# Norms of a two-stage transformer kernel: one over the root on 64 columns, spread over the partitions by small products

## The chip, the core and the metric

The kernel runs on one core of a Trainium2 chip. A core has a matrix engine (TensorE, PE in the profile; its weight loads are PEld), a vector engine (VectorE, DVE), a scalar engine (ScalarE, ACT), GpSimd (POOL) and a sync engine (SyncE, SP), with 16 DMA engines behind the queues. Each engine runs its own instructions in order and waits for the others by semaphores. The metric is the device time of one execution in microseconds (us); the number quoted is the median of the runs shown.

## The reference

One sequence of T = 256 tokens with D = 1024 features passes a first block (a modulated norm, a mixer of a Fourier part and a gated delta rule over tokens and a context, a gated feed-forward with a convolution) and then two layers (attention, retention and a linear recurrence side by side, then a feed-forward). Between all of these stand root-mean-square norms over the 1024 features of each token:

```
def rms_norm(x, g):
    xf = x.astype(jnp.float32)
    y = xf * lax.rsqrt(jnp.mean(xf * xf, axis=-1, keepdims=True) + EPS)
    return (y * g.astype(jnp.float32)).astype(x.dtype)
```

There are 13 of them in the kernel, numbered k = 0 to 12: 0 and 1 on the two inputs, then pairs. The first of a pair (2, 4, 6, 8, 10, and 12 alone at the end) normalises the output of a branch, which is then scaled and added to x ("residual norm"); the second (3, 5, 7, 9, 11) normalises the new x for the next branch ("modulate norm").

## The kernel before

Activations lie transposed: `[P, KT, T]`, that is 128 partitions, 8 blocks of 128 features, 256 tokens. Weights stream in through a ring of slots in chunks of 128x2048 fp32 (1 MB, `raw`), by SP's queue. ACT copies each chunk to a rounded `w_hi` (L1059) and DVE subtracts to get `w_lo` (L1590, 2.29 us a chunk); PE then multiplies in three products per tile (`mm3`, L342 to L344), 48 matmuls a chunk. There are two buffers of `w_hi` and `w_lo`, so the preparation of chunk n+2 starts when chunk n is done. The order of the work on each engine is written out by hand; the only things that order engines against each other are semaphores.

A norm runs over four engines' worth of code. ACT squares two blocks at a time (`square`, L1100, 128x512). For each of the four pairs of blocks PE multiplies by `omean`, a 128x128 matrix with 1/1024 in every place (`norm_part`, L446), so that after eight products all 128 partitions of PSUM bank 7 hold the mean of squares of all 256 tokens: the sum over the partitions and its spreading over them are one step. ACT takes the root of 128x256 with eps (`root`, L1105, tile `std`). DVE takes the reciprocal of 128x256 (L1619 in `rs`, L1637 in `root_done`, tile `rstd`) and multiplies by it: `residual` (L1667 from PSUM, then L1675 into x), `modulate` (L1653, with L1654 for the low part behind ACT's L1125), `rs` for norms 0 and 1 (L1624), and L1967 for norm 3. Each of the first three parts of a residual norm stands between two weight chunks in PE's order; the fourth stands behind the last chunk.

Behind a norm PE has filler work, in its order ahead of the next thing that waits: `keep_warm` (L457, products of 512 columns whose results nobody reads: 4 before and 4 behind norms 7 and 11, likewise around norm 9, 2 in front of norm 3, 2 behind norm 5) and `ada_mm` (L467, products with the modulation weights, 16 matmuls of 32 weight columns for each 1 MB half that POOL's queue loads into one of two buffers; the next load into a buffer waits until it has been used). After a modulate norm PE's next chunk (`mod_chunk`, `up_chunk`) waits block by block for the modulated activations.

Of the kernel before, what the change touches and what calls it, by code (L numbers as in the profile page):

```python
# [90 lines left out]
def build_program(nc, io, layers=LAYERS):  # L91
# [6 lines left out]
    with ctx:  # L98
# [239 lines left out]
        def _(pe):  # L338
# [1242 lines left out]
        def _(dve):  # L1581
# [159 lines left out]
            def conv_kv(c):  # L1741
                dve.wait_ge(S("evicted"), c + 3)
                for i in range(3):
                    for b in (2 * c, 2 * c + 1):
# [721 lines left out]
```

## Time and profile before

| | |
|---|---|
| median of 3 runs | 1807.72 us (1801.07 to 1809.67) |
| the profiled execution | 1812.65 us, of which its span 1810.8 us |
| mean granted TensorE clock | 0.981 |
| PE busy | 1709.5 us (94%) |
| DVE busy | 1097.9 us (61%) |
| ACT busy | 811.7 us (45%) |
| reciprocals of 128x256 | 13, each 1.75 us |
| means by L446 | 13 x 8 matmuls |

The span is from the first to the last instruction; the time of a run lies 1.85 us above it here. A matmul of fp32 data is recorded as two (x16 rows for the 8 matmuls of a norm). Busy time of PE counts a matmul from its start to its modelled end, so that 94% is no measure of what PE could not do. Idle time in brackets behind a row is that of the engine before it, with what ended it.

### The profile page before, as it was taken

The page shows a single profiled execution, that of the slowest core. Times are in us where ns is not written, and L with a number is a line of the kernel's source. Part 1 is how long each engine was busy: PE and PEld are TensorE (multiplying, and loading weights), DVE is VectorE, ACT ScalarE, POOL GpSimd, SP SyncE. Part 2 cuts the span into 40 slices and gives each one's busy share as a digit, 9 for nine tenths or more (in the row PEclk, how much of TensorE's full clock was granted, in tenths as well). Part 3 has the DMA queues.
Part 4 walks back from the last instruction along what each step waited for, and adds up shares of the span by engine and source line. Part 5 has one row for each costly group of instructions (what it writes and reads, how often), then busy time and mean ns, then how long its engine had stood idle before and what let it go on. Part 6 is the DMA issues. An engine that isn't in the chain of part 4 may idle for free.

```text
span 1810.8 us, 34649 instructions
## 1 busy us (share of the span) xinstructions
PE 1709.5 (94%) x15394; PEld 1607.6 (89%) x15394; DVE 1097.9 (61%) x1367; ACT 811.7 (45%) x1050; POOL 34.2 (2%) x68
## 2 busy tenths in 40 slices
PE   6998788899989799999999999999999999999997
PEld 4797688789979599999999799979999999979997
DVE  4466753579953554477785664565547778666463
ACT  3245413343333344445754444435364575445352
POOL 0000000000000000000000000000000000000000
PEclk8999999999989899999999999999999999999999
DMA  9676442555558553445455355535444445535551
GB/s 401 241 269 255 160 182 94 188 212 175 173 189 300 210 171 138 140 163 185 165 187 181 112 195 188 188 115 185 134 150 160 163 166 186 188 113 188 196 198 71
DMA packets 45210, 329.32 MB, mean 182 GB/s; under 512 B 5008, under 2 KB 5008, under 8 KB 5392
## 3 DMA queue, kind: packets, MB, share of 16 engines
q1 hardware_dynamic: 35712, 258.63, 41.2%
q0 software_dynamic: 9216, 67.11, 9.8%
q8 instruction: 114, 1.87, 0.4%
q10 hardware_dynamic: 144, 1.51, 0.2%
q14 instruction: 24, 0.20, 0.0%
HBM read 326.18 MB, written 1.05 MB: 181 GB/s over the span
## 4 chain that ended last, share of the span: by engine, by line
PE 76%; DVE 11%; ACT 7%; DMA 4%; issue 1%; SPq 0%; POOL 0%; ACTq 0%; DVEq 0%
PE ps L342 19%; PE ps L343 19%; PE ps L344 19%; DVE w_lo L1590 4%; PE ps L395 4%; ACT w_hi L1059 3%; PE ps L467 3%; DMA ada_raw<-ada 2%; PE ps L446 2%; DMA raw<-stream 2%; PE ps L627 1%; PE ps L638 1%; DVE rstd L1637 1%; DVE rsq L2309 1%; DVE x L1675 1%
## 5 line engine op out<-in xcount | busy, mean ns | idle before, releaser
L1590 DVE TENSOR_TENSOR w_lo<-raw,w_hi 128x2048 fp32r<-128x2048 f32 x207 | 474.4, 2292 | 501.4 <-ACT w_hi L1059 501.0
L342 PE MATMUL ps<-act_hi,w_hi 128*128 128x256 f32 x2672 | 757.7, 284 | 18.1 <-DVE act_lo L1632 5.0
L343 PE MATMUL ps<-act_lo,w_hi 128*128 128x256 f32 x2672 | 745.7, 279 | 0.0
L344 PE MATMUL ps<-act_hi,w_lo 128*128 128x256 f32 x2672 | 745.6, 279 | 0.0
L1059 ACT ACTIVATE w_hi<-raw 128x2048 fp32r<-128x2048 f32 (+1 forms) x229 | 421.8, 1842 | 568.9 <-PE ps L344 559.4
L342 PEld LDWEIGHTS ps<-act_hi,w_hi 128*128 128x128 f32 x2672 | 505.6, 189 | 29.1 <-issue 16.5
L343 PEld LDWEIGHTS ps<-act_lo,w_hi 128*128 128x128 f32 x2672 | 505.2, 189 | 1.1 <-issue 0.2
L344 PEld LDWEIGHTS ps<-act_hi,w_lo 128*128 128x128 f32 x2672 | 504.4, 189 | 0.0
L342 PE MATMUL ps<-mlp_hi,w_hi 128*128 128x256 f32 x512 | 142.9, 279 | 0.4
L343 PE MATMUL ps<-mlp_lo,w_hi 128*128 128x256 f32 x512 | 141.4, 276 | 0.0
L344 PE MATMUL ps<-mlp_hi,w_lo 128*128 128x256 f32 x512 | 141.4, 276 | 0.0
L342 PEld LDWEIGHTS ps<-mlp_hi,w_hi 128*128 128x128 f32 x512 | 96.1, 188 | 1.1 <-DVE w_lo L1598 1.0
L2006 DVE SCALAR_TENSOR_TENSOR gacc<-gpad,vectors,gacc 128x256 f32<-128x256 f32 x176 | 84.6, 481 | 19.8 <-ACT gacc L1327 14.7
L343 PEld LDWEIGHTS ps<-mlp_lo,w_hi 128*128 128x128 f32 x512 | 96.1, 188 | 0.2
L344 PEld LDWEIGHTS ps<-mlp_hi,w_lo 128*128 128x128 f32 x512 | 96.2, 188 | 0.0
L467 PE MATMUL ps<-ada_raw,silu_c_wide 128*32 128x256 f32 x1024 | 67.4, 400 | 21.4 <-DMA ada_raw<-ada 21.3
L395 PE MATMUL ps<-h_up,raw 128*128 128x256 f32 x352 | 82.3, 386 | 1.6 <-ACT h_up L1317 1.3
L395 PEld LDWEIGHTS ps<-h_up,raw 128*128 128x128 f32 x352 | 65.4, 192 | 13.2 <-ACT h_up L1317 3.0
L467 PEld LDWEIGHTS ps<-ada_raw,silu_c_wide 128*32 128x32 f32 x1024 | 30.1, 113 | 47.8 <-DMA ada_raw<-ada 27.4
L342 PE MATMUL ps<-w_hi,act_hi 128*128 128x256 f32 x256 | 72.2, 282 | 0.0
L344 PE MATMUL ps<-w_hi,act_lo 128*128 128x256 f32 x256 | 71.3, 279 | 0.0
L343 PE MATMUL ps<-w_lo,act_hi 128*128 128x256 f32 x256 | 71.3, 278 | 0.0
(404 smaller groups left out, 2053.5 us busy)
## 6 DMA issues: line engine op xcount, KB each, us to landing
raw<-stream SPq DMA_DIRECT2D x233, 1024.0 KB, 4.9
ada_raw<-ada POOLq DMA_DIRECT2D x64, 1024.0 KB, 6.9
ada_f<-ada SPq DMA_DIRECT2D x4, 1024.0 KB, 12.8
ada_a<-ada SPq DMA_DIRECT2D x3, 1024.0 KB, 19.8
consts_stage<-consts_a SPq DMA_DIRECT2D x1, 1728.0 KB, 33.7
consts_stage<-consts_b ACTq DMA_DIRECT2D x1, 1472.0 KB, 8.9
x<-xT SPq DMA_DIRECT2D x1, 1024.0 KB, 5.8
xc<-ctxT SPq DMA_DIRECT2D x1, 1024.0 KB, 7.8
```

The lines of the kernel that those rows point to most:

```text
L342: mm(out, ah, bh, start=first, stop=False, skip_group_check=shared)
L343: mm(out, ah, bl, start=False, stop=False, skip_group_check=shared)
L344: return mm(out, al, bh, start=False, stop=last, skip_group_check=shared)
L395: mm(ps[:, bank, 0:T], raw[:, slot, k * P:(k + 1) * P], h_up[:, k, :], start=k == 0, stop=k == KT - 1)
L446: last = mm(ps[:, 7, 0:T], omean, sq[:, b, :], start=b == 0, stop=b == KT - 1)
L467: last = mm(ps[strip:strip + 32, bank, c * T:(c + 1) * T], cs_wide[:, k, 32 - 3 * j:64 - 3 * j], ada_raw[:, c, k * T:(k + 1) * T], start=j ...
L627: last = mm(ps[r:r + 64, INV_BANK[q], j * 64:(j + 1) * 64], B01[d][r:r + 64, t0 + j // 4, j % 4, r:r + 64], Tm[r:r + 64, q, j, :], start=T ...
L638: last = mm(ps[r:r + 64, INV_BANK[q], j * 32:(j + 1) * 32], Uc[r:r + 64, q, j, :], half(X[r:r + 64, q, j, :], d, 1 << lvl), start=True, st ...
L1059: act_(w_hi[:, s2, o:CH], raw[:, s4, o:CH], ACT.Copy).then_inc(S("hi_ready"), 1)
L1590: tt(w_lo[:, s2, :], raw[:, s4, :], w_hi[:, s2, :].bitcast(f32), ALU.subtract).then_inc(S("lo_ready"), 1)
L1637: nc.vector.reciprocal(rstd[:, :], std[:, :]).then_inc(S("norm_rstd"), 1)
L2006: ins = stt(acc, src, w, acc, ALU.mult, ALU.add)
```

## The change

The 256 tokens are cut in four quarters of 64. In `norm_part` each block is multiplied in four matmuls of 32 weight columns and 64 data columns; quarter i goes to PSUM partitions 32i to 32i+31, columns 0 to 63 of bank 7. Every partition of a strip of 32 then holds the means of that strip's quarter. Root and reciprocal work on 128x64 (`std[:, 0:64]`, `std[:, 64:128]`). Then four matmuls, each with one column of the identity (the column of partition 32i) repeated 128 times as weights, take row 32i of the reciprocals and spread it over all 128 partitions, to columns 256 + 64i of bank 7. These four stand in PE's order right behind the last part of the mean, with a wait for DVE's reciprocal ahead of them. Residual norms and norms 0 and 1 copy the 128x256 result to `rstd` first (`root_done`); modulate norms read it in PSUM (`root_row`). Four semaphores are merged into two (`eps_set` and `cs_ready` into `consts_set`; `conv` and `y_ready` into `kqv_done`), and PE's second norm waits for `norm_rstd` in place of `norm_std`.

```diff
-                    last = mm(ps[:, 7, 0:T], omean, sq[:, b, :], start=b == 0, stop=b == KT - 1)
+                    for i in range(4):
+                        last = mm(ps[32 * i:32 * i + 32, 7, 0:64], omean[:, 0:32], sq[:, b, 64 * i:64 * i + 64],
+                                  start=b == 0, stop=b == KT - 1, skip_group_check=True)
                 if q == 3:
                     last.then_inc(S("norm_ms"), 1)
+                    pe.wait_ge(S("norm_inv"), k + 1)
+                    for i in range(4):
+                        last = mm(ps[:, 7, T + 64 * i:T + 64 * i + 64], ident[:, 32 * i:32 * i + 1].to_broadcast([P, P]), std[:, 64:128],
+                                  start=True, stop=True)
+                    last.then_inc(S("norm_row"), 1)
...
             norm(0, norm_sq1)
-            pe.wait_ge(S("norm_std"), 1)
+            pe.wait_ge(S("norm_rstd"), 1)
...
-                act_(std[:, :], ps[:, 7, 0:T], ACT.Sqrt, bias=eps[:, :]).then_inc(S("norm_std"), 1)
+                act_(std[:, 0:64], ps[:, 7, 0:64], ACT.Sqrt, bias=eps[:, :]).then_inc(S("norm_std"), 1)
...
+            def root_row(k):
+
+                dve.wait_ge(S("norm_std"), k + 1)
+                nc.vector.reciprocal(std[:, 64:128], std[:, 0:64]).then_inc(S("norm_inv"), 1)
+                dve.wait_ge(S("norm_row"), k + 1)
+                return ps[:, 7, T:2 * T]
+
+            def root_done(k):
+
+                row = root_row(k)
+                copies[0] += 1
+                nc.vector.tensor_copy(rstd[:, :], row).then_inc(S("norm_rstd"), 1)
+                dve.wait_ge(S("norm_rstd"), copies[0])
...
-            def root_done(k):
-
-                dve.wait_ge(S("norm_std"), k + 1)
-                nc.vector.reciprocal(rstd[:, :], std[:, :]).then_inc(S("norm_rstd"), 1)
-                dve.wait_ge(S("norm_rstd"), k + 1)
...
-                root_done(k)
-                pipe(m, lambda b: stt(tmp[:, b, :], src[:, b, :], g[:, b:b + 1], rstd[:, :], ALU.mult, ALU.mult),
+                row = root_row(k)
+                pipe(m, lambda b: stt(tmp[:, b, :], src[:, b, :], g[:, b:b + 1], row, ALU.mult, ALU.mult),
```

PE's order around norms 6 and 7 (end of the mixer of the first layer), before; L342 to L344 are the last products of the last weight chunk, L446 the means, L457 `keep_warm`, and the last rows the first chunk of the feed-forward:

```order
L344 MATMUL ps<-act_hi_53,w_lo 128x256
L446 MATMUL ps<-s_136,consts_common 128x256 x4
L457 MATMUL ps<-consts_common 128x512 x4
L446 MATMUL ps<-s_136,consts_common 128x256 x8
L457 MATMUL ps<-consts_common 128x512 x4
L342 MATMUL ps<-act_hi_54,w_hi 128x256
```

The same place in the changed kernel; L447 are the means, L453 the four spreading products (they wait for DVE), L464 `keep_warm`:

```order
L344 MATMUL ps<-act_hi_53,w_lo 128x256
L447 MATMUL ps<-s_136,consts_common 32x64 x16
L453 MATMUL ps<-std,consts_common 128x64 x4
L464 MATMUL ps<-consts_common 128x512 x4
L447 MATMUL ps<-s_136,consts_common 32x64 x32
L453 MATMUL ps<-std,consts_common 128x64 x4
L464 MATMUL ps<-consts_common 128x512 x4
L342 MATMUL ps<-act_hi_54,w_hi 128x256
```

Each `keep_warm` now stands behind a wait for the reciprocal. The same happens to `ada_mm` around norms 4 and 5; before (L467 is `ada_mm`):

```order
L446 MATMUL ps<-sq_down,consts_common 128x256 x2
L467 MATMUL ps<-ada_raw,silu_c_wide 32x256 x32
L446 MATMUL ps<-s_136,consts_common 128x256 x8
L467 MATMUL ps<-ada_raw,silu_c_wide 32x256 x16
L457 MATMUL ps<-consts_common 128x512 x2
```

and after (L474 is `ada_mm`):

```order
L447 MATMUL ps<-sq_down,consts_common 32x64 x8
L453 MATMUL ps<-std,consts_common 128x64 x4
L474 MATMUL ps<-ada_raw,silu_c_wide 32x256 x32
L447 MATMUL ps<-s_136,consts_common 32x64 x32
L453 MATMUL ps<-std,consts_common 128x64 x4
L474 MATMUL ps<-ada_raw,silu_c_wide 32x256 x16
L464 MATMUL ps<-consts_common 128x512 x2
```

Here the loads that refill the two buffers of `ada_mm` hang on it too. DVE's order around norms 6 and 7, after (L1636 is the copy, L1597 the low part of a weight chunk, and L1668 reads its last operand in PSUM):

```order
L1628 RECIPROCAL std<-std 128x64
L1636 COPY rstd<-ps 128x256
L1682 TENSOR_TENSOR s_135<-ps,rstd 128x512 x2
L1690 SCALAR_TENSOR_TENSOR x<-s_135,gain_scale,x 128x256 x2
...
L1597 TENSOR_TENSOR w_lo<-raw,w_hi 128x2048
L1628 RECIPROCAL std<-std 128x64
L1668 SCALAR_TENSOR_TENSOR s_135<-x,gain_scale,ps 128x256 x3
```

The low part of a weight chunk stands ahead of the second reciprocal, as before the change.

## Rows read from the trace of the kernel before

**Rows 1.** The page, busy time of each engine over the whole span.

```profile
PE 1709.5 (94%) x15394; PEld 1607.6 (89%) x15394; DVE 1097.9 (61%) x1367; ACT 811.7 (45%) x1050; POOL 34.2 (2%) x68
```

**Rows 2.** Chain that ended last (start us, us, what), the end of the first block.

```profile
595.96 10.86 DMA ada_raw<-ada
606.87 1.94 PE ps L467 x16
608.81 4.49 PE ps L446 x16
613.89 1.76 DVE rstd L1637
615.68 1.28 DVE s L1653 x3
```

**Rows 3.** Timeline of norms 6 and 7 (start us, us, instruction, [idle before]).

```profile
1004.95 1.98 PE L446 MATMUL ps<-s,consts_common 128*128 128x256 f32 x8
1005.15 0.60 ACT L1100 ACTIVATE s<-ps 128x512 f32<-128x512 f32 x1 [2.35 <-PE ps L344]
1006.97 0.47 ACT L1105 ACTIVATE std<-ps,eps 128x256 f32<-128x256 f32 x1 [1.22 <-PE ps L446]
1007.48 1.75 DVE L1637 RECIPROCAL rstd<-std 128x256 f32<-128x256 f32 x1 [4.34 <-ACT std L1105]
1009.26 1.29 DVE L1667 TENSOR_TENSOR s<-ps,rstd 128x512 f32<-128x512 f32 x2
1014.95 2.29 DVE L1590 TENSOR_TENSOR w_lo<-raw,w_hi 128x2048 fp32r<-128x2048 f32 x1
1016.67 3.60 PE L457 MATMUL ps<-consts_common 128*128 128x512 f32 x8
1017.37 1.75 DVE L1637 RECIPROCAL rstd<-std 128x256 f32<-128x256 f32 x1
1019.16 1.28 DVE L1653 SCALAR_TENSOR_TENSOR s<-x,gain_scale,rstd 128x256 f32<-128x256 f32 x3
1020.98 0.35 PE L342 MATMUL ps<-act_hi,w_hi 128*128 128x256 f32 x1 [0.72 <-DVE act_lo L1654]
1027.28 1.92 ACT L1059 ACTIVATE w_hi<-raw 128x2048 fp32r<-128x2048 f32 x1 [2.33 <-PE ps L344]
```

**Rows 4.** Timeline of ACT at the start of the kernel.

```profile
37.31 1.91 ACT L1059 ACTIVATE w_hi<-raw 128x2048 fp32r<-128x2048 f32 x1 [1.48 <-DMA raw<-stream]
```

**Rows 5.** Groups by shape (busy us, mean ns of one, idle before).

```profile
L1686 DVE RECIPROCAL smalls<-smalls 128x32 f32<-128x32 f32 x1 | 0.4, 352 | 0.0
L1794 DVE COPY smalls<-ps 128x64 f32<-128x64 f32 x1 | 0.2, 217 | 0.0
L1898 DVE COPY U<-ps 128x512 f32<-128x512 f32 x8 | 5.4, 690 | 10.1 <-PE ps L698 10.1
L627 PE MATMUL ps<-Tm,Bm 64*64 64x64 f32 x640 | 20.4, 219 | 4.7 <-issue 4.7
L1094 ACT ACTIVATE junk<-eps 128x1 f32<-128x1 f32 x6 | 1.2, 197 | 0.0
```

**Rows 6.** Timeline of PE: eight full-width products of two columns.

```profile
27.61 1.05 PE L511 MATMUL ps<-strip_rows,mod_rows 128*128 128x2 f32 x8
```

**Rows 7.** Timeline of PE: one mean part, and strips of 32, between weight products.

```profile
341.18 1.02 PE L446 MATMUL ps<-norm_sq,consts_common 128*128 128x256 f32 x4
341.85 0.47 PE L342 MATMUL ps<-act_hi,w_hi 128*128 128x256 f32 x1
...
648.00 1.07 PE L485 MATMUL ps<-s,small_wide 128*32 128x256 f32 x16
649.00 0.38 PE L342 MATMUL ps<-act_hi,w_hi 128*128 128x256 f32 x1
```

**Rows 8.** Windows around norm 9; the clock is the number behind the engines.

```profile
1208.00:1210.00 2.00, 2.00 (x6) 1.49 (x6) 1.08 (x3) 1.26 (x2) 0.00 (x0) 0.50 0.00 0
1210.00:1212.00 2.00, 2.00 (x8) 1.62 (x7) 0.00 (x0) 0.00 (x0) 0.00 (x0) 0.70 0.00 0
```

More of the change, by code:

```diff
@@ L496, in _ @@
             norm(0, norm_sq1)
-            pe.wait_ge(S("norm_std"), 1)
+            pe.wait_ge(S("norm_rstd"), 1)
             norm(1, norm_sq1)
-            pe.wait_ge(S("cs_ready"), 1)
+            pe.wait_ge(S("consts_set"), 2)
             for m in range(ADA_FIRST):
@@ L546, in _ @@
                     ada_mm(6 + c // 2)
-            pe.wait_ge(S("y_ready"), 1)
+            pe.wait_ge(S("kqv_done"), 2)
             for g in range(6):
@@ L1150, in _ @@
             act_(cth[:, :], vec[:, 0:3 * KT], ACT.Tanh, scale=0.5).then_inc(S("c_tanh"), 1)
-            act.wait_ge(S("eps_set"), 1)
+            act.wait_ge(S("consts_set"), 1)
             act.wait_ge(S("x_loaded"), 16)
@@ L1190, in _ @@
             job(N_UZ, N_UZ, 1, lambda i: flat(uz[:, 2 * i:2 * i + 2, :]))
-            act.wait_ge(S("conv"), 1)
+            act.wait_ge(S("kqv_done"), 1)
             act_(th_kv[:, :, :, :], y_kv[:, :, :, :], ACT.Tanh, scale=0.5)
@@ L1614, in job @@
                     four(r, min(4, count - r))
+            copies = [0]
+            def root_row(k):
[8 more added lines that the diff above has]
+                dve.wait_ge(S("norm_rstd"), copies[0])
             def rs(k, src, dst):
-                dve.wait_ge(S("norm_std"), k + 1)
-                nc.vector.reciprocal(rstd[:, :], std[:, :]).then_inc(S("norm_rstd"), 1)
-                dve.wait_ge(S("norm_rstd"), k + 1)
+                root_done(k)
                 marks = []
@@ L1694, in softplus @@
                 order(stt(dst, e, 2.0, m, ALU.mult, ALU.add))
-            nc.vector.memset(eps[:, :], EPS).then_inc(S("eps_set"), 1)
+            nc.vector.memset(eps[:, :], EPS).then_inc(S("consts_set"), 1)
             dve.wait_ge(S("c_tanh"), 1)
@@ L1704, in _ @@
             dve.wait_ge(S("cc_loaded"), 16)
-            red(sel[:, :], ident.rearrange("p (s r) -> p r s", s=4), AX, ALU.add).then_inc(S("cs_ready"), 1)
-            dve.wait_ge(S("cs_ready"), 1)
+            red(sel[:, :], ident.rearrange("p (s r) -> p r s", s=4), AX, ALU.add).then_inc(S("consts_set"), 1)
+            dve.wait_ge(S("consts_set"), 2)
             marks = [rs(0, x, norm_h1)]
@@ L1748, in conv_kv @@
                         if b == 7 and i == 2:
-                            ins.then_inc(S("conv"), 1)
+                            ins.then_inc(S("kqv_done"), 1)
                         else:
@@ L1790, in _ @@
             order(stt(flat(y_q[:, :, :]), flat(th_q[:, :, :]), 1.0, flat(y_q[:, :, :]), ALU.add, ALU.mult))
-            stt(flat(y_kv[:, :, :, :]), flat(th_kv[:, :, :, :]), 1.0, flat(y_kv[:, :, :, :]), ALU.add, ALU.mult).then_inc(S("y_ready"), 1)
+            stt(flat(y_kv[:, :, :, :]), flat(th_kv[:, :, :, :]), 1.0, flat(y_kv[:, :, :, :]), ALU.add, ALU.mult).then_inc(S("kqv_done"), 1)
             dve.wait_ge(S("gc_mm"), 1)
@@ L1965, in _ @@
             prep(N_UP + 1, (N_UP + 1) % RAW, (N_UP + 1) % 2)
-            root_done(3)
-            pipe(2, lambda b: stt(norm_h1[:, b, :], x[:, b, :], gs[:, 1, b:b + 1], rstd[:, :], ALU.mult, ALU.mult),
+            row3 = root_row(3)
+            pipe(2, lambda b: stt(norm_h1[:, b, :], x[:, b, :], gs[:, 1, b:b + 1], row3, ALU.mult, ALU.mult),
                  lambda b: tt(act_lo[1][:, b, :], h_up[:, b, :], act_hi[1][:, b, :].bitcast(f32), ALU.subtract))
```

3 lines of the change are left out of this document (removed).

## The prediction

> **What bounds the kernel now.** I read the page first. PE is busy 94% of the span and nothing else passes 61% [rows 1]: PE's stream of weight chunks is the bound, and a norm costs what it makes that stream wait. The chain of waits says where: PE and DVE pieces of the norms stand on it at each of the five pairs, as at norms 4 and 5 [rows 2]. The timeline of one pair [rows 3] gives the steps. Residual norm 6: last square ends 1005.75, root starts 1006.97 (1.22 later), reciprocal 1007.48, multiply 1009.26. Modulate norm 7: the reciprocal starts at 1017.37, but DVE was held by the low part of a weight chunk until 1014.95 + 2.29 = 1017.24; the first multiply comes at 1019.16, PE's chunk starts at 1020.98 and is done by 1027.28, where ACT starts what waits for it.
>
> **Prices.** (a) Tail of the mean, last square to root. Sixteen records (8 matmuls, each recorded twice) at the pitch of the nearest small products, 20.4/640 = 0.032 us (L627, [rows 5]), the last lasting 0.22, with 0.05 + 0.04 of hand-over as in the gaps of rows 3: 0.05 + 15 x 0.032 + 0.22 + 0.04 = 0.79 against 1.22, so -0.43. From above, strips of 256 columns take 1.07 for 16 (L485, [rows 7]): then -0.06. (b) Root: 0.47 on 256 columns, 0.20 on one [rows 3, 5]; for 64 I take 0.33, between both, -0.14. (c) Reciprocal: 352 ns at 32 columns, 1753 at 256 [rows 5, 3], 6.25 ns a column, 0.55 at 64: -1.20. (d) New: reciprocal to multiply was 0.03; now the hand-over to PE, eight records with full-width weights, and the way back. Eight such records with two data columns take 1.05 [rows 6]; weights, not data, set that pitch, so 64 columns add little: 0.05 + 1.08 + 0.04 = 1.17, hence +1.14. Bounds: 8 x 0.032 + 0.2 = 0.46 if a repeated column loaded like narrow weights, and twice 1.05 at half clock. (e) Copy, residual norms only: 217 ns at 64 columns, 690 at 512 [rows 5], 0.42 at 256, with its hand-over +0.45. Reading the row in PSUM instead of SBUF in the modulate multiplies I cost at nothing; the 512-column multiply reads PSUM already (1.29 for two), bounds 0 to 0.1 each.
>
> A residual norm: -0.43 - 0.14 - 1.20 + 1.14 + 0.45 = -0.18. A modulate norm whose reciprocal waits for the low part of a chunk anyway (norms 3, 7, 11) gains neither tail nor root, only 1017.37 - 1017.28 = 0.09: -0.09 - 1.20 + 1.14 = -0.15 at DVE.
>
> **By place.**
> Norms 0, 1: 2 us earlier or more, worth 0: ACT's second weight copy waits for DMA until 37.31 [rows 4], and no activation is rounded before it.
> Norms 2, 3: 0 (-0.4 to +0.9): DVE is 0.3 earlier, but `ada_mm` now follows the spreading and makes `up_chunk` start about 0.8 later, against a chunk fed block by block.
> Norms 6, 7 and 10, 11: queued behind PE's new wait are `keep_warm` and then the chunk. Before, `keep_warm` ran 1016.67 to 1020.27, under root and reciprocal, and the chunk waited 0.72 more for DVE. Now the reciprocal is ready at 1017.28 + 0.55 = 1017.83 (less 0.18 from norm 6), spreading ends at 18.96, and `keep_warm` runs behind it until about 1022.2, while DVE's first block is ready at 1020.7. The chunk is 48 products at 0.114 = 5.5: before it was fed by DVE and took 1020.98 to 1027.2, now it runs unfed from 1022.2 and ends at 1027.7 to 1028.0. So the DVE gain is lost and PE is +0.6 late, twice: +1.2 (-0.3 to +2).
> Norms 8, 9: no weight chunk stands before this reciprocal, so tail, root and reciprocal all count, -1.9 and -0.18 at full clock. Half of that is in doubt: PE's clock was at its lower level there (0.50 in 1208 to 1210, [rows 8]), which lengthens (a) and (d). I take -1.2 (-2.0 to +0.5).
> Norms 4, 5: `ada_mm` behind norm 4 starts some 1.8 later (root to spread row), and the loads that refill its buffers with it; the second landed at 606.87 and PE waited for it [rows 2]. With 1 MB streams beside it I take +0.6 of the 1.8. Then the mean of norm 5, 4.49 for 16 records at mixed clock, becomes 64 records, some 2.6: -1.9, root and reciprocal and spreading -0.2, and `keep_warm` gives part back. I take -0.8 (-1.5 to +1.5).
> Norm 12: -0.2 to the last multiply.
> Sum: +1.2 - 1.2 - 0.8 - 0.2 = -1.0.
>
> **Parts inside the stream.** Fifteen mean parts stand between weight products, where PE is the bound. The cost of one: the next weight product starts 0.67 late and runs 0.19 longer (341.85, [rows 7]): 0.86. New: 16 x 0.032 = 0.51, and something for going from full width to strips and back: the strip products of rows 7 hold PE from 647.9 to 649.22, 1.2, of which 16 x 0.058 is work: 0.27. Together 0.78, -0.08 each, -1.2 in all. Bounds: no charge for the change of width, -0.35 each, -5; strips as slow as those of 256 columns, 1.2, +0.34 each, +5. The Trainium skill ("TensorEngine Tiling (Array Packing)", section "Key Properties") says that changing the tiling mode drains the engine; by it the 0.27 is paid at every part; the trace agrees, with that 0.27.
>
> **Clock.** Before, norm 9 shows what thin PE work does: after a pause and mean parts with gaps the granted clock was 0.50 for 1208 to 1210 and 0.70 over the next 2, that is the lower of the two levels, 1.2 GHz, for about 3.3 us [rows 8], worth 3.3/2 = 1.65 us of work. Norm 7 with the same pattern kept 2.4 GHz. Now each part between `keep_warm` and spreading is 0.7 busy instead of 1.1, and PE then waits 1.5 more. I expect one more such fall at norms 7 and 11, in one of the two: +1.6 (0 to +8 over five modulate norms).
>
> **Forecast.** -1.0 - 1.2 + 1.6 = -0.6 against the profiled 1812.65 (span 1810.8 and 1.85 around it), so 1812.0; the median shown is 4.9 below that execution: 1807.72 - 0.6 = 1807.
>
> **Rivals.**
> A, faster (0.2). Narrow products leave no charge at the change of width and the clock holds: -5 in the stream, -2.5 at the places: 1800, or 1797 at the ends of both bounds. For it: L627's small products ran dense at 2.4 GHz. Against: 0.27 at the one place where strips follow weights.
> B, slower by a new clock fall (0.17). Mechanism: `keep_warm` exists to keep PE at 2.4 GHz, and it now stands behind a wait, with thin parts ahead. Once the fall comes before the spreading, spreading is 1 us longer and `keep_warm` and the chunk lose 1.65 more: 2.6 at each of norms 3, 5, 7, 9, 11, +13 and no gain anywhere: 1820. It decides if the fall comes at three of them. For it: norm 9 already falls. Against: norms 7 and 11 do not, with gaps of 1.7 us.
> C, strips of 64 columns no faster than strips of 256 (0.1): +5 in the stream, -0.06 in place of -0.43 in the tails and 2 more at norm 5, with the places' +0: about +9 on the forecast, 1816.
> The change not doing what it says, the repeated column loading slowly (0.03): +1 at each of 11 norms, 1818.
> The forecast itself has 0.5, with 1803 to 1812 of its own.
>
> **Range and chances.** Half a per cent, 9 us, is about what a measurement of this kernel tells from no change. Range 1799 to 1817. Faster by more: the far half of A, 0.1. Slower by more: B's cases with three falls or more, and half of C and the last, 0.14. Within: 0.76.
>
> **What would show it.** Reciprocals 0.55 and roots about 0.33; spreading products as x8 in 1.1 us; L447 parts 16 records in 0.5 between weight products, with the next weight product about 0.8 late; at norm 7 `keep_warm` ending after DVE's first low part, and the chunk starting at its end without idle time for DVE; the clock in windows ahead of each `keep_warm`. Wrong if the norms' rows gain and the chunk behind them starts earlier than before, or if the parts inside the stream cost less than 0.5.

## The result, and the profile after

| | kernel before | changed kernel |
|---|---|---|
| median of 18 runs each, us | 1808.45 (1801.07 to 1813.46) | 1815.72 (1808.39 to 1823.48) |
| profiled execution, us | 1812.65 | 1813.72 |
| its span, us | 1810.8 | 1811.9 |
| its mean granted clock | 0.981 | 0.977 |

The ratio is 1.0037, with a 95% interval of 1.0024 to 1.005: slower by 0.24 to 0.5%, where the forecast was 1807.0 (-0.03%). 1815.7 lies inside the range of 1799 to 1817, and the loss is inside the half per cent that the prediction called no change, but the sign is not the forecast's. In a second session, told below, the same kernel came to 1.0016 (0.9995 to 1.0037), which takes in no change. The two profiled executions are only 1.1 us apart: that of the kernel before lies 4.2 above its median and that of the changed kernel 2.0 below. The traces can thus show where time moved, but not all of the 7.3 us between the medians.

The page's line of busy time, against [rows 1]: PE has 728 records more and 4 us less work.

```profile
PE 1705.6 (94%) x16122; PEld 1601.9 (88%) x16122; DVE 1085.1 (60%) x1375; ACT 810.1 (45%) x1050; POOL 34.2 (2%) x68
```

Norms 6 and 7 again, in the timeline (start us, us, instruction, [idle before]), against [rows 3]:

```profile
1004.71 0.43 PE L447 MATMUL ps<-s,consts_common 128*32 128x64 f32 x16 [0.33 <-ACT s L1107]
1005.21 0.31 ACT L1112 ACTIVATE std<-ps,eps 128x64 f32<-128x64 f32 x1 [0.55 <-PE ps L447]
1005.55 0.55 DVE L1628 RECIPROCAL std<-std 128x64 f32<-128x64 f32 x1 [3.40 <-ACT std L1112]
1006.16 1.10 PE L453 MATMUL ps<-std,consts_common 128*128 128x64 f32 x8 [1.02 <-DVE std L1628]
1007.30 0.42 DVE L1636 COPY rstd<-ps 128x256 f32<-128x256 f32 x1 [1.20 <-PE ps L453]
...
1013.45 2.29 DVE L1597 TENSOR_TENSOR w_lo<-raw,w_hi 128x2048 fp32r<-128x2048 f32 x1
1014.13 0.43 PE L447 MATMUL ps<-s,consts_common 128*32 128x64 f32 x16 [0.36 <-ACT s L1107]
1015.65 0.55 DVE L1628 RECIPROCAL std<-std 128x64 f32<-128x64 f32 x1
1016.26 1.97 PE L453 MATMUL ps<-std,consts_common 128*128 128x64 f32 x8 [1.70 <-DVE std L1628]
1018.02 5.44 PE L464 MATMUL ps<-consts_common 128*128 128x512 f32 x8
1018.26 1.26 DVE L1668 SCALAR_TENSOR_TENSOR s<-x,gain_scale,ps 128x256 f32<-128x256 f32 x3 [2.06 <-PE ps L453]
1022.89 0.68 PE L342 MATMUL ps<-act_hi,w_hi 128*128 128x256 f32 x1
```

The small steps came out as priced or better: root 0.31 (0.33), reciprocal 0.55 (0.55), spreading 1.10 at norm 6 (1.10), copy 0.42 (0.42), last square to root 0.55 (0.79). But at norm 7 the eight records of the spreading take 1.97, and `keep_warm` behind them 5.44, not 3.60. The windows of the same place say why; the number behind the engines is the granted clock:

```profile
1014.00:1016.00 2.00, 0.43 (x16) 0.27 (x16) 2.00 (x2) 0.39 (x2) 0.00 (x0) 0.70 0.04 8
1016.00:1018.00 2.00, 1.74 (x8) 1.75 (x9) 0.20 (x1) 0.00 (x0) 0.00 (x0) 0.50 0.00 0
1018.00:1020.00 2.00, 2.00 (x5) 0.97 (x5) 1.74 (x5) 1.22 (x3) 0.00 (x0) 0.50 0.00 0
1020.00:1022.00 2.00, 2.00 (x4) 0.74 (x3) 2.00 (x6) 1.18 (x4) 0.00 (x0) 0.60 0.00 0
```

PE was busy 0.43 of the 2 us from 1014. The clock fell to 1.2 GHz near 1014.8 and was back at 2.4 GHz near 1021.6 (worked out from the 0.70 and 0.60 of the first and last window). The chunk starts at 1022.89, 4.63 us behind the first multiply at 1018.26, where it was 1.82 [rows 3]. Before the change the window of the same place was:

```profile
1014.00:1016.00 2.00, 1.74 (x8) 1.22 (x7) 1.97 (x4) 1.26 (x2) 0.00 (x0) 1.00 0.00 0
```

From here on, "shortfall" is the work at full speed that PE could not do because the clock was at its lower level, summed over windows of 2 us. It is 3.4 us here, and as much at norm 11; at norm 9 it is 1.7, as before.

Inside the stream (PE's timeline, against [rows 7]) the weight product behind a mean part now starts 0.57 after the one ahead of it, 0.45 late at a pitch of 0.12, and runs 0.11 longer: 0.56 in all, where it was 0.86.

```profile
340.54 0.28 PE L344 MATMUL ps<-act_hi,w_lo 128*128 128x256 f32 x1
340.75 0.43 PE L447 MATMUL ps<-norm_sq,consts_common 128*32 128x64 f32 x16
341.11 0.39 PE L342 MATMUL ps<-act_hi,w_hi 128*128 128x256 f32 x1
```

At norms 4 and 5 the chain of waits (start us, us, what), against [rows 2]: PE waits for the two transfers that `ada_mm` uses until 612.67, and its two `keep_warm` products take 3.71 at 1.2 GHz, all of it on the chain.

```profile
594.19 7.38 DMA ada_raw<-ada
...
606.00 6.63 DMA ada_raw<-ada
612.67 1.94 PE ps L474 x16
614.60 3.71 PE ps L464 x4
```

**How the places are compared from here on.** ACT's rounding of a weight chunk (`w_hi`) starts when PE has finished an older chunk, so it marks PE's progress. For each pair of norms I take the time between such a start ahead of the pair (at 329.68, 580.29, 992.56, 1181.30, 1582.73 in the kernel before) and one behind it (373.04, 630.31, 1027.28, 1229.18, 1623.42), minus the same in the kernel before: us, one profile each. The ratios are each to executions of the kernel before in the same session; kernels of different sessions, in part also of different chips, are compared by these ratios alone. e6_odd and e9_mix1 rest on 6 executions and e11_not1 on 8, the others on 11 to 18.

| kernel | ratio to before (95%) | 2/3 | 4/5 | 6/7 | 8/9 | 10/11 | sum |
|---|---|---|---|---|---|---|---|
| changed kernel | 1.0037 (1.0024 to 1.005) | -0.4 | +1.9 | +2.6 | -2.9 | +2.5 | +3.5 |
| the same, r_again | 1.0016 (0.9995 to 1.0037) | -1.2 | -1.6 | +3.0 | -0.4 | +1.4 | +1.2 |
| e1_fill | 0.9985 (0.9964 to 1.0007) | +0.4 | -1.4 | +1.3 | -2.7 | -0.5 | -2.9 |
| e2_short | 0.9976 (0.9957 to 0.9995) | -1.0 | -4.5 | +0.1 | -1.9 | -0.8 | -8.2 |
| e3_both | 0.9976 (0.9957 to 0.9995) | +0.5 | -2.9 | +0.1 | -1.6 | -0.1 | -4.0 |
| the same, r_both | 0.9955 (0.9932 to 0.9978) | +0.4 | -2.6 | -1.2 | -2.9 | -1.4 | -7.6 |
| e4_wait_only | 1.0067 (1.0043 to 1.009) | +1.6 | +0.1 | +2.5 | -0.7 | +0.9 | +4.3 |
| e5_even | 1.0008 (0.9989 to 1.0027) | 0.0 | +0.7 | -0.8 | -1.2 | -1.3 | -2.6 |
| e6_odd | 1.0073 (1.0053 to 1.0093) | +0.7 | -1.0 | +2.9 | +1.3 | +3.7 | +7.6 |
| e7_mix | 0.9976 (0.996 to 0.9992) | -0.8 | -2.2 | -0.3 | -2.7 | -1.1 | -7.0 |
| the same, r_mix | 0.998 (0.9962 to 0.9998) | +0.2 | -2.4 | -0.8 | -1.2 | -1.3 | -5.4 |
| e8_short5 | 1.001 (0.9995 to 1.0026) | -0.3 | +0.1 | +2.6 | -2.7 | +1.4 | +1.0 |
| e9_mix1 | 1.005 (1.003 to 1.0069) | -0.7 | -0.2 | -0.8 | +0.3 | -1.2 | -2.6 |
| the same, r_mix1 | 0.9974 (0.9949 to 0.9998) | -0.8 | -0.1 | -0.8 | -1.4 | -1.1 | -4.3 |
| e10_even1 | 1.001 (0.9994 to 1.0026) | -0.8 | -1.8 | -0.2 | -1.4 | -0.5 | -4.7 |
| e11_not1 | 1.0073 (1.0048 to 1.0098) | -1.1 | +0.2 | +1.7 | -0.1 | +2.3 | +3.0 |

Twice the same kernel differs by up to 3.5 us at pair 4/5, by up to 2.6 at 8/9, and by 1.3 or less at 6/7 and 10/11.

### The profile page after: what moved, and what is told of

It reads as the page before. It is cut to its first block, busy times and chain, and to the rows that moved or that the text cites. A ratio compares the mean times of both kernels' runs of the same rounds, so it can differ in the third digit from the quotient of the medians.

```text
span 1811.9 us, 36113 instructions
## 1 busy us (share of the span) xinstructions
PE 1705.6 (94%) x16122; PEld 1601.9 (88%) x16122; DVE 1085.1 (60%) x1375; ACT 810.1 (45%) x1050; POOL 34.2 (2%) x68
## 3 DMA queue, kind: packets, MB, share of 16 engines
q8 instruction: 120, 1.97, 0.4%
## 4 chain that ended last, share of the span: by engine, by line
PE 77%; DVE 10%; ACT 7%; DMA 4%; issue 2%; SPq 0%; POOL 0%; ACTq 0%; DVEq 0%; POOLq 0%
PE ps L342 20%; PE ps L344 19%; PE ps L343 19%; DVE w_lo L1597 4%; PE ps L395 4%; ACT w_hi L1066 3%; DMA ada_raw<-ada 3%; PE ps L474 3%; DMA raw<-stream 1%; PE ps L634 1%; PE ps L645 1%; PE ps L464 1%; DVE x L1690 1%; DVE rsq L2324 1%; PE ps L453 1%
## 5 line engine op out<-in xcount | busy, mean ns | idle before, releaser
L1597 DVE TENSOR_TENSOR w_lo<-raw,w_hi 128x2048 fp32r<-128x2048 f32 x207 | 474.5, 2292 | 509.0 <-ACT w_hi L1066 508.6
L342 PE MATMUL ps<-act_hi,w_hi 128*128 128x256 f32 x2672 | 756.9, 283 | 15.3 <-DVE act_lo L1674 5.3
L344 PE MATMUL ps<-act_hi,w_lo 128*128 128x256 f32 x2672 | 745.4, 279 | 0.0
L342 PEld LDWEIGHTS ps<-act_hi,w_hi 128*128 128x128 f32 x2672 | 504.8, 189 | 24.2 <-issue 12.9
L344 PEld LDWEIGHTS ps<-act_hi,w_lo 128*128 128x128 f32 x2672 | 505.0, 189 | 0.0
L342 PE MATMUL ps<-mlp_hi,w_hi 128*128 128x256 f32 x512 | 142.9, 279 | 0.4
L344 PE MATMUL ps<-mlp_hi,w_lo 128*128 128x256 f32 x512 | 141.9, 277 | 0.0
L342 PEld LDWEIGHTS ps<-mlp_hi,w_hi 128*128 128x128 f32 x512 | 96.5, 188 | 1.5 <-DVE w_lo L1605 1.0
L344 PEld LDWEIGHTS ps<-mlp_hi,w_lo 128*128 128x128 f32 x512 | 96.2, 188 | 0.0
L474 PE MATMUL ps<-ada_raw,silu_c_wide 128*32 128x256 f32 x1024 | 69.7, 411 | 21.8 <-DMA ada_raw<-ada 21.8
L474 PEld LDWEIGHTS ps<-ada_raw,silu_c_wide 128*32 128x32 f32 x1024 | 30.7, 115 | 48.1 <-DMA ada_raw<-ada 27.4
L342 PE MATMUL ps<-w_hi,act_hi 128*128 128x256 f32 x256 | 72.1, 282 | 0.0
L344 PE MATMUL ps<-w_hi,act_lo 128*128 128x256 f32 x256 | 71.2, 278 | 0.0
```

Of the source, the lines that this page charges most:

```text
L342: mm(out, ah, bh, start=first, stop=False, skip_group_check=shared)
L344: return mm(out, al, bh, start=False, stop=last, skip_group_check=shared)
L474: last = mm(ps[strip:strip + 32, bank, c * T:(c + 1) * T], cs_wide[:, k, 32 - 3 * j:64 - 3 * j], ada_raw[:, c, k * T:(k + 1) * T], start=j ...
L1597: tt(w_lo[:, s2, :], raw[:, s4, :], w_hi[:, s2, :].bitcast(f32), ALU.subtract).then_inc(S("lo_ready"), 1)
```

## The experiments

**Theory O (order).** `keep_warm` stands behind PE's wait for the reciprocal, and so on the path between the multiplies and the chunk. **Theory C (clock).** The narrow means and PE's pause let the clock fall, and everything behind them runs at half speed.

**e1_fill**: filler products where PE had become thin.

```
+                if q < 2 and k in (3, 7, 9, 11):
+                    keep_warm(1, 4 if k == 3 else 6)
                 if q == 3:
                     last.then_inc(S("norm_ms"), 1)
+                    keep_warm({3: 2, 7: 2, 11: 2, 9: 1}.get(k, 0), ...)
                     pe.wait_ge(S("norm_inv"), k + 1)
```

> The changed kernel, with full-width filler products (each 0.9 us at the higher clock) put where PE's work had become thin: one behind each of the first two mean parts of norms 3, 7, 9 and 11, and two (norm 9: one) ahead of PE's wait for the reciprocal. Clock theory (the clock falls to 1.2 GHz in norms 5, 7 and 11 because PE idles more there, and doubles the spreading, 1.97 for 1.10, and keep_warm, 5.44 for 3.60): the granted clock stays at its upper level from 1014 to 1022 and at norm 11, spreading 1.1 and keep_warm 3.6 at norms 7 and 11, the chunk behind each starts 2.0 to 2.6 earlier than in the changed kernel; -4 to -6 us against it, ratio to before 0.999 to 1.002. Rival, the order theory (what costs is only that keep_warm stands behind the wait for DVE, whatever the clock): fillers change nothing or cost up to 1 us, ratio 1.003 to 1.005.

Measured: 0.9985, mean clock 0.984. The timeline, `keep_warm` of norm 6 first, then norm 7:

```profile
999.87 5.35 PE L467 MATMUL ps<-consts_common 128*128 128x512 f32 x8
...
1008.57 1.98 PE L467 MATMUL ps<-consts_common 128*128 128x512 f32 x4
1009.05 0.55 DVE L1631 RECIPROCAL std<-std 128x64 f32<-128x64 f32 x1 [0.55 <-ACT std L1115]
1010.39 1.00 PE L456 MATMUL ps<-std,consts_common 128*128 128x64 f32 x8
1011.22 3.65 PE L467 MATMUL ps<-consts_common 128*128 128x512 f32 x8
1014.31 0.68 PE L342 MATMUL ps<-act_hi,w_hi 128*128 128x256 f32 x1
```

Spreading 1.00 and `keep_warm` 3.65 at norm 7: the clock held there, and pair 6/7 lost 1.3 and not 2.6 to 3.0, pair 10/11 gained 0.5. Of the 2 to 2.6 expected at each, 1.3 and 3.0 came. Two fillers are a little too long here: they end at 1010.4, 0.8 behind the reciprocal. Theory C has a share. Whether order has one this run doesn't say: the 1.3 left at pair 6/7 is no more than two profiles of one kernel differ by, and the clock fell here too, one norm earlier (1.7 us of shortfall between 1000 and 1004). `keep_warm` behind norm 6, which also stands behind a wait now, took 5.35 for it, and the reciprocal of norm 7 waited 0.55 for the root. At norms 10 and 11 the clock didn't fall, and the pair was 0.5 shorter than before.

**e2_short**: `keep_warm` behind the modulate norms cut.

```
                 if L == 0:
                     ada_mm(31)
-                    keep_warm(2, 0)
                 else:
-                    keep_warm(4, 6)
+                    keep_warm(1, 6)
...
-                keep_warm(4, 6)
+                keep_warm(1, 6)
```

> The changed kernel, with the keep_warm products behind the modulate norms' spreading cut: one for four at norms 7, 9, 11, none for two at norm 5. Order theory (keep_warm is 3.6 to 5.4 us of work that now stands on the path between spreading and chunk): the chunk is fed by DVE again and starts 1.2 to 2.6 earlier at each of norms 7 and 11, as much at 5 and 9; -5 to -8 us, ratio to before 0.999 to 1.001. Clock theory: the chunk starts earlier but its first products run at 1.2 GHz until the clock is back, so what keep_warm no longer costs the chunk pays: -2 to +1 us against the changed kernel, ratio 1.002 to 1.004.

Measured: 0.9976, and the mean clock stays low, 0.976 in the profile. The timeline of norm 7, then the windows there:

```profile
1013.27 1.97 PE L453 MATMUL ps<-std,consts_common 128*128 128x64 f32 x8 [1.70 <-DVE std L1627]
1015.03 2.02 PE L464 MATMUL ps<-consts_common 128*128 128x512 f32 x2
1017.09 0.55 PE L342 MATMUL ps<-act_hi,w_hi 128*128 128x256 f32 x1
```

```profile
1014.00:1016.00 2.00, 2.00 (x8) 1.48 (x7) 0.72 (x2) 0.20 (x1) 0.00 (x0) 0.50 0.00 0
1016.00:1018.00 2.00, 1.97 (x6) 0.94 (x5) 2.00 (x6) 1.61 (x4) 0.00 (x0) 0.50 0.00 0
1018.00:1020.00 2.00, 2.00 (x16) 2.00 (x15) 2.00 (x6) 1.29 (x3) 0.00 (x0) 0.79 0.00 0
```

This is the telling run. The clock fell at norm 7 as far as in the changed kernel, and the pair cost nothing (+0.1). The chunk's first products ran at 1.2 GHz for under 2 us, and PE caught up: DVE delivers a block each 0.79 us, and at full clock its six products take 6 x 0.114 = 0.68. So theory C's forecast ("what keep_warm no longer costs the chunk pays") is wrong, and so is O alone, since fillers helped with `keep_warm` left in place. Both are one mechanism: a fall costs time because `keep_warm`, four products queued behind the wait, is stretched by it. Without the fall, or without the four products, most of the loss goes. The twelve executions say the same as the trace: their clocks are 0.973 to 0.978, as low as the changed kernel's 0.971 to 0.979, and their median is below that of the kernel before.

**e3_both**: both edits, run in two sessions (the second as r_both).

> Both edits together: fillers ahead of the wait, keep_warm behind it cut. If both causes hold, each with its share, the gains add: clock at its upper level through norms 7 and 11, chunk fed by DVE right behind the multiplies, and what the narrow products save inside the stream (15 x 0.29 = 4.3 us) is left: ratio to before 0.995 to 0.998, faster than both kernels. If only the clock counts: as the fill run, 0.999 to 1.002. If neither: 1.003.

> e3_both once more (fillers, keep_warm cut). Ratio 0.9957 to 0.9995 again if it is the kernel's own; pairs 6/7 and 10/11 within 0.5 of the kernel before, pair 8/9 -1.5, the clock at its upper level at norm 11 and at the lower for at most 1.7 us of lost work at norms 7 and 9.

Measured: 0.9976 and 0.9955, faster than both kernels. The gains do not add at norms 7 and 11 (+0.1, -0.1; then -1.2, -1.4): either edit is enough. The 1.2 us by which the two profiles differ goes with the clock again: in the first it fell at norms 6 and 10 (1.7 us of shortfall each, where the expectation had it at its upper level), in the second at neither. One comparison needs no ratio across sessions: r_both and the changed kernel (r_again) ran in the same one, with medians of 1806.7 and 1813.64. The timeline of norm 7 in the second session: fillers end with the reciprocal, one `keep_warm`, and the chunk starts as DVE's first block is ready.

```profile
1007.07 1.98 PE L467 MATMUL ps<-consts_common 128*128 128x512 f32 x4
1008.88 1.05 PE L456 MATMUL ps<-std,consts_common 128*128 128x64 f32 x8
1009.77 1.08 PE L467 MATMUL ps<-consts_common 128*128 128x512 f32 x2
1011.78 0.36 PE L342 MATMUL ps<-act_hi,w_hi 128*128 128x256 f32 x1 [0.93 <-DVE act_lo L1671]
```

**e4_wait_only**: the kernel before, with only the wait.

```
                 if q == 3:
                     last.then_inc(S("norm_ms"), 1)
+                    pe.wait_ge(S("norm_rstd"), k + 1)
```

> The kernel before, full-width means, root and reciprocal on all 256 columns, no spreading, but PE waits for the reciprocal behind the mean of every norm, so keep_warm and ada_mm stand behind the wait as in the changed kernel. Reciprocal and root are longer than in the changed kernel (1.75 and 0.47 for 0.55 and 0.31), so PE's pause is longer. If the place of keep_warm and ada_mm behind a wait is what makes the change slow: slower than before by 2.5 to 5 us at each of norms 5, 7, 9, 11, ratio 1.005 to 1.011. If the narrow products themselves are the cause (thin work), the wait alone costs what PE is late at norms 7 and 11, 1 us each: ratio 1.000 to 1.002.

Measured: 1.0067, with full-width means and no spreading. Pair 6/7 is 2.5 longer, 10/11 0.9, 2/3 1.6. The timeline, `keep_warm` of norm 6 first, then norm 7:

```profile
1010.03 5.40 PE L458 MATMUL ps<-consts_common 128*128 128x512 f32 x8 [2.35 <-DVE rstd L1638]
...
1019.43 1.75 DVE L1638 RECIPROCAL rstd<-std 128x256 f32<-128x256 f32 x1 [1.44 <-ACT std L1106]
1021.24 3.70 PE L458 MATMUL ps<-consts_common 128*128 128x512 f32 x8 [2.35 <-DVE rstd L1638]
1024.37 0.68 PE L342 MATMUL ps<-act_hi,w_hi 128*128 128x256 f32 x1
```

At full clock, as at norm 7 here, `keep_warm` behind the wait already holds the chunk until 1024.37, 3.15 behind the first multiply at 1021.22; before it was 1.82 (1019.16 to 1020.98, [rows 3]): 1.33 for the order. The rest of pair 6/7 goes with the clock: PE idled 2.35 at norm 6's wait, the clock fell (1.7 us of shortfall between 1010 and 1014), `keep_warm` behind it took 5.40, and norm 7's reciprocal waited 1.44 for the root. At pair 10/11 there was no fall, and the wait cost 0.9, the 1 us that the expectation's rival had for it. The profile is also one of the shorter executions of this kernel (1816.67, median 1822.23): the four shortest have clocks of 0.981 to 0.983, the four longest 0.974 to 0.978. So the wait alone costs what the whole change costs or more, but 1.0067 is no price of order alone. Nor does the run separate what lets the clock fall: with wide means it fell at norm 6 and held at norms 7 and 11, and no run has narrow means without a wait.

**e5_even and e6_odd**: the change at the even norms alone (first, residual and last), and at the odd, modulate norms alone. The other norms keep the full mean, root and reciprocal, and no wait. Of the edit only the choice of the means is shown; root, reciprocal, spreading and the counts of the waits follow it.

```
+                narrow = k % 2 == 0        # e6_odd: k % 2 == 1
                 for b in (2 * q, 2 * q + 1):
+                    if not narrow:
+                        last = mm(ps[:, 7, 0:T], omean, sq[:, b, :], start=b == 0, stop=b == KT - 1)
+                        continue
```

> The change at the residual and first norms alone (0, 2, 4, 6, 8, 10, 12); the modulate norms 1, 3, 5, 7, 9, 11 keep the full mean, root and reciprocal and PE doesn't wait in them. Theory (the loss stands at the modulate norms, where keep_warm stands behind the wait; the even norms gain): clock as before, 0.981, keep_warm 3.6 under the reciprocal at norms 7 and 11, the chunk behind each pair 0.2 to 1.0 earlier than before, the parts inside the stream 0.29 cheaper each; -3 to -6 us, ratio to before 0.997 to 0.9985. Rival (the narrow products themselves cost something wherever they stand in the stream, which the profile's rows hide): ratio 1.000 or above.

> The change at the modulate norms alone (1, 3, 5, 7, 9, 11); the even norms, and with them all mean parts inside the weight stream, are as before. Theory: all of the loss and none of the gain in the stream; norms 7 and 11 +2.5 each, 5 +2, 9 -2.5, clock 0.976: +4 to +9 us, ratio 1.002 to 1.005. Rival: ratio 0.999 to 1.001.

Measured: 1.0008 and 1.0073, 6.5 thousandths apart in one session. The five pairs say the same, -2.6 and +7.6: the loss stands at the modulate norms. That the residual norms and the stream gain is in the rows alone (norm 6 in 3.1 for 3.5, a part in 0.56 for 0.86): the median of e5_even is where the rival of its expectation put it, at 1.000 or above. Both ratios are 2 to 3 thousandths above what the pairs give (-2.6 and +7.6 us of 1812), and both traces have 4.5 to 5.8 us more ahead of norm 2, which e9 to e11 follow up.

**e7_mix** (again as r_mix): narrow at the even norms and at 5 and 9, full at 1, 3, 7 and 11; `keep_warm` behind norm 5 cut, fillers at norm 9.

> The change where its places gained in the traces: at the even norms and at 5 and 9; norms 1, 3, 7 and 11, whose reciprocal waits for the low part of a chunk anyway, stay full. keep_warm behind norm 5 is cut, and norm 9 has one filler product behind each of its first two mean parts and one ahead of PE's wait. Theory: what e5_even gives (-3 to -6), -2.5 at norm 9 and -2 to -4 at norm 5: -7 to -11 us, ratio 0.994 to 0.997, clock 0.981 or above. Rival (the wait at norms 5 and 9 costs what the reciprocal gains): as e5_even.

> e7_mix once more (narrow at the even norms, 5 and 9). If a kernel's ratio is its own, 0.996 to 0.999 as before; if sessions differ by as much as e7_mix and e9_mix1 did, anything from 0.995 to 1.005.

Measured: 0.9976 and 0.998. The size is short of the -7 to -11, the direction is the forecast's, and it repeats. The clock is 0.98 and 0.978 in the two profiles, not 0.981 or above. At norm 7, with full means, `keep_warm` again runs under root and reciprocal, and the chunk starts 1.82 behind the first multiply, as before. (The 0.71 in front of the reciprocal is again a fall at norm 6, 1.7 us of shortfall; r_mix has none there.)

```profile
1015.87 3.60 PE L478 MATMUL ps<-consts_common 128*128 128x512 f32 x8
1016.58 1.75 DVE L1644 RECIPROCAL rstd<-std 128x256 f32<-128x256 f32 x1 [0.71 <-ACT std L1126]
1018.37 1.28 DVE L1690 SCALAR_TENSOR_TENSOR s<-x,gain_scale,rstd 128x256 f32<-128x256 f32 x3
1020.19 0.35 PE L342 MATMUL ps<-act_hi,w_hi 128*128 128x256 f32 x1 [0.72 <-DVE act_lo L1691]
```

**e8_short5**: the changed kernel without the two `keep_warm` products at norm 5.

> The changed kernel with one edit: the two keep_warm products behind ada_mm at norm 5 left out. At half clock they took 3.71 us on the chain ahead of the chunk. If norms 4 and 5 are where the order costs most (the trace of e2_short has that pair 6.3 us shorter than the changed kernel's): -3 to -5 us against the changed kernel, ratio to before 1.001 to 1.002. If that was the ada transfer's own chance in those two profiles: -1 at most, ratio 1.003 to 1.004.

Measured: 1.001. Against the changed kernel's two ratios that is -0.6 to -2.7 thousandths, -1 to -5 us; in between what the two theories had. The interval (0.9995 to 1.0026) holds the first theory's 1.001 to 1.002 and not the second's 1.003 to 1.004, but that figure was worked out from the 1.0037 alone, and against the 1.0016 the products are worth 1 us. Pair 4/5 itself is +0.1, between the changed kernel's own two profiles (+1.9 and -1.6). Not settled.

**e9_mix1, e10_even1, e11_not1**: the same kernels with norm 1 changed over, an edit that the expectations hold to be worth nothing at its place. e9 and r_mix1 are e7_mix, e10 is e5_even, with norm 1 narrow; e11 is the changed kernel with norm 1 full.

> The mixed kernel e7_mix with norm 1 narrow as well. At norm 1 the change itself is worth nothing (that stage waits for DMA), but PE's instructions up to norm 3 are then the same in number as in the changed kernel. The traces of e5_even, e6_odd and e7_mix, where norm 0 or 1 was full, have a pause of PE with no releaser of about 2.65 us near 227 us (1.39 to 1.65 in the kernel before and the changed one) and 1.2 GHz for 13 us behind it, far from any norm: about +5 us by norm 2. Theory of the pause (its place and length follow from how many instructions PE has had, so it goes with the instruction count): the pause is 1.7 or less, no fall near 228, and the ratio is 0.995 (0.993 to 0.9965). Rival (the long pause was chance or that chip's): as e7_mix, 0.9975.

> e5_even with norm 1 narrow as well: the change at the even norms and at norm 1. Same reasoning: without the long pause near 227 us the ratio is 0.998 (0.9965 to 0.999), -2 to -6 us, which is what the even norms and the fifteen parts inside the stream are worth; if the long pause is chance, as e5_even, 1.001; if the narrow parts in the stream gain nothing, 1.000 even without the pause.

> The changed kernel with norm 1 alone made full again, an edit that should be worth nothing at its own place. Theory of the pause: PE's instructions up to norm 3 are now as many as in e5_even with one difference, so the long pause and 13 us at 1.2 GHz appear near 227 us: +4 to +6 against the changed kernel, ratio 1.006 to 1.007. Rival: no change, ratio 1.003 to 1.004.

> e9_mix1 once more (as e7_mix, norm 1 narrow too). If the ratio is the kernel's own: 1.003 to 1.007, and then its second profile, if it is a typical run, shows where 10 us go that the first (its shortest run) does not have. If it was chance: 0.994 to 0.998.

Measured: 1.005 (then 0.9974), 1.001, 1.0073. In the traces the theory of the pause holds in part. The windows of e5_even behind its pause, its first product behind it, and the same product in the changed kernel:

```profile
228.00:230.00 2.00, 0.62 (x12) 0.63 (x14) 0.00 (x0) 0.00 (x0) 0.00 (x0) 0.73 0.00 0
230.00:232.00 2.00, 2.00 (x18) 1.88 (x14) 0.69 (x1) 0.00 (x0) 0.00 (x0) 0.50 0.03 8
```

```profile
229.38 1.12 PE L645 MATMUL ps<-Tm,Bm 64*64 64x64 f32 x16 [2.65 <-issue]
```

```profile
232.19 0.97 PE L634 MATMUL ps<-Tm,Bm 64*64 64x64 f32 x26 [1.65 <-issue]
```

All five profiles of kernels in which just one of norms 0 and 1 is narrow (e5, e6, e7, r_mix, e11) have the clock at its lower level near 230 to 245, a shortfall of 3.4 to 6.8 us, and 2.3 to 5.8 us more ahead of norm 2 than the kernel before (between the starts of rounding that the kernel before has at 48.32 and 298.13). The ten others with both norms narrow, and e4 with neither, have none there, and lie between -5.7 and +0.7. But the pause was not always long (1.56 in r_mix, 1.83 in e11), so its length alone does not decide. And the ratios bear it out only at e11, as forecast. e10, whose trace has no such fall, has the ratio of e5: by the expectation either the pause costs nothing in the median or the narrow parts gain nothing, and the runs don't tell which. e9 in its first session lies 7 thousandths above e7, which ran in an earlier one on another chip; in the one session that had both (r_mix, r_mix1) they are equal. So the effect is in the traces, and its worth in the median is open.

**r_again**: the changed kernel itself in another session.

> The changed kernel itself once more, for a second profile and a second ratio. If its loss is its own: ratio 1.0024 to 1.005, the clock again at its lower level for 3.4 us of lost work at norms 7 and 11 and not longer than 1.7 at norm 9, pairs 6/7 and 10/11 again +2.5, pair 8/9 again -2.9. If the loss was that session's: ratio 0.998 to 1.002.

Measured: 1.0016 (0.9995 to 1.0037), mean clock 0.976. The clock fell again at norms 7 and 11, and here at norm 9 as well (3.4 in all); 6/7 cost +3.0, 10/11 +1.4, 8/9 -0.4, where +2.5, +2.5 and -2.9 were expected. The timeline of norm 7:

```profile
1011.64 1.97 PE L453 MATMUL ps<-std,consts_common 128*128 128x64 f32 x8 [1.70 <-DVE std L1628]
1013.40 6.02 PE L464 MATMUL ps<-consts_common 128*128 128x512 f32 x8
1018.85 0.68 PE L342 MATMUL ps<-act_hi,w_hi 128*128 128x256 f32 x1
```

The mechanism repeats. The ratio does so only in part: 1.0016 lies in what the expectation gave to "that session's" loss (0.998 to 1.002), not in 1.0024 to 1.005. The loss is 0.16 to 0.37% over two sessions, and e9_mix1 against r_mix1 warns that sessions can differ by more than their intervals say.

**All profiles together.** What four `keep_warm` products behind a wait and a fall of the clock cost can be read over the whole table:

| at norms 7 and 11 | profiles | 6/7 | 10/11 |
|---|---|---|---|
| narrow, four products, the clock falls | changed kernel, r_again, e6, e8, e11 | +1.7 to +3.0 | +1.4 to +3.7 |
| narrow, four products, no fall there | e1 | +1.3 | -0.5 |
| narrow, one product, fall or none | e2, e3, r_both | -1.2 to +0.1 | -1.4 to -0.1 |
| wide, no wait | e5, e7, r_mix, e9, r_mix1, e10 | -0.8 to -0.2 | -1.3 to -0.5 |

The first row is apart from the third and the fourth by more than two profiles of one kernel differ.

## Why the prediction was wrong, point by point

**What bounds the kernel**: right. PE is busy 94% of the span in both kernels, and the pairs' sums go with the ratios.

**Prices (a) to (e)**: right at full clock, with one mis-sized. Pitch of the narrow mean records: 0.032 taken, (0.43 - 0.22)/15 = 0.014 measured. So a tail is 0.55, not 0.79. Reading the row in PSUM cost nothing, as taken (1.26 for three multiplies, before 1.28). A residual norm at norm 6 runs from last square to first multiply in 0.55 + 0.31 + 0.03 + 0.55 + 0.06 + 1.14 + 0.46 = 3.1, against 3.5 before (1.22 + 0.51 + 1.78, [rows 3]): -0.4 where -0.18 stood.

**Parts inside the stream**: mis-sized, in the change's favour. Before, a chunk with a part took 6.32 and one without 5.44, 0.88 for the part (0.86 taken). In the changed kernel the chunk with the last part of norm 12 in it takes 6.03 at the same pace, 0.59, where 0.78 was forecast: -0.29 each, not -0.08. The term that was off is the pitch: sixteen records are 16 x 0.014 = 0.22 of work and not 0.51. The charge for the change to strips and back was there, and a little larger than the 0.27 taken: 0.56 - 0.22 = 0.34. In the rows it is 0.09 ahead of the first narrow record (0.21 behind the weight product for 0.12), 0.14 behind the last, and the 0.11 by which the next weight product is longer. The Trainium skill ("TensorEngine Tiling (Array Packing)", section "Key Properties") says that a change of tiling mode drains TensorE; the trace agrees, with that 0.34 at each part.

**The step that failed: norms 6, 7, 10, 11 and the clock.** It read: `keep_warm` "runs behind it until about 1022.2", +0.6 at each pair, and "I expect one more such fall at norms 7 and 11, in one of the two: +1.6". Together +2.8 for the two pairs. Measured: falls at both norms, in both profiles of the kernel, 3.4 us of shortfall each and not 1.65 (in the second profile the 3.4 of pair 10/11 is 1.7 at norm 10 and 1.7 at norm 11); `keep_warm` ended at 1023.46; +5.1 and +4.3 for the two pairs. Two things were wrong in it. The fall was held to be a chance, weighed by norm 9 alone, although the prediction itself had PE's work ahead of the wait thinner and the wait longer; PE was busy 0.43 us in the 2 from 1014, and a part was 0.43 long where 0.7 was taken. And the price of a fall was taken as the work not done in it, wherever it falls. e2_short shows that it depends on what stands there: nothing where DVE feeds the chunk and PE can catch up, most of it where `keep_warm` is queued behind the wait. The +0.6 for the order alone is neither borne out nor refuted: with the clock at its upper level pair 10/11 was +0.9 in e4_wait_only (with a longer reciprocal) and -0.5 in e1_fill (with fillers).

**Norms 8, 9**: -1.2 (-2.0 to +0.5) forecast; -2.9 and -0.4 measured, the second with a second fall: one outside the range and one inside. The "-1.9" behind the forecast leaves out the spreading; by the prices (a) to (d) it is -0.43 - 0.14 - 1.20 + 1.14 = -0.63 at norm 9, and with norm 8's -0.18 only -0.8.

**Norms 4, 5**: -0.8 (-1.5 to +1.5) forecast, +1.9 and -1.6 measured, one just outside either end. `keep_warm` "gives part back" was wrong in the first, where it took 3.71 at half clock on the chain. The pair depends on when two transfers of 1 MB land, and its spread is larger than the term.

**Norms 2, 3**: 0 (-0.4 to +0.9) forecast; -0.4 and -1.2.

**Sum**: -4.4 in the stream, of which the pairs' intervals hold a part, and +3.5 or +1.2 over the pairs: that is at most -1 to -3, while the ratios say +6.7 and +2.9 us. So the traces place a loss of 4 to 5 us at two pairs, and the experiments show what takes it away, but the balance of the medians isn't closed. The traces' own balance is: the spans of the changed kernel's two profiles are +1.1 and -1.4 against that of the kernel before, which is +3.5 and +1.2 at the pairs and -2.4 and -2.6 elsewhere. What the other executions spend beyond that no trace covers; stretches that differ by as much between two runs of one kernel are known (the last section). That the measured 1815.7 lies inside the range of 1799 to 1817 is no credit to the working: it is 1.3 from the end where the cases of B begin.

**Rivals.** B described the mechanism, for `keep_warm`; that the chunk too loses by the fall is what e2_short excludes at norm 7. At its size, 2.6 each, it stood at two of its five norms, and at norm 5 the shortfall was 6.8 where it had been 5.1; its point of decision, "if the fall comes at three of them", was not quite met, and the outcome of the first session lies between the forecast and B. A's gain in the stream came nearly true as well (-0.29 a part for its -0.35), by cheaper records and not, as A had it, by a missing charge; both happened at once. C fell: strips of 64 columns have a pitch of 0.014.

## What to carry to other kernels

A keep-busy filler belongs ahead of a wait, where it runs in time that is idle anyway; the same filler behind the wait is on the path, and a clock fall stretches it (3.60 to 5.44 and 6.02). When a change makes an engine's small work cheaper, ask what that work was also doing: here the wide means had kept PE busy 1.74 us of the 2 in which the narrow ones kept it busy 0.43. Steps whose result waits for another engine's earlier work anyway (mean and root at norms 3, 7 and 11, which wait for the low part of a chunk) gain nothing from being made faster; e7_mix left these norms as they were and kept the gain elsewhere.

## What was not expected of the hardware

- A clock fall can cost nothing where PE is fed by a slower engine and catches up: at norm 7 of e2_short the shortfall was 3.4 us and the pair was +0.1 us.
- Weight chunks run at one of two paces at full granted clock, 5.44 or 5.65 us, mostly in stretches of some 6 to 14 chunks, at other places in each run: 47 slow chunks in the profile before, about 45 after, and about 50 in r_again. Each is 0.21 us longer, so a stretch moves a run by 1 to 3 us, with no cause that the traces show.
- Sixteen records of 64 columns on strips of 32 take 0.43 us, a pitch of 0.014; four of 256 columns at full width take 1.02 [rows 7]. Going to strips and back between weight products cost 0.34 beside that.
- PE has pauses without a releaser between 205 and 257 us (about 1 to 2.65 us each), whose places move from kernel to kernel; the clock fell behind the one near 230 in all five profiles of kernels in which just one of norms 0 and 1 is narrow, and in none of the twelve others.
- Two sessions, on two chips, gave one kernel 1.005 (1.003 to 1.0069) and 0.9974 (0.9949 to 0.9998): below half a per cent, one session does not settle a ratio here. Whether the chip or the session makes the difference is open.
